# Fourteen experts on 64 slots with both parts of their tokens in one stationary tile, and gelu in one ScalarE pass

## What is computed

```python
logits = xf @ router_w + router_b            # 512 tokens, 32 experts
top_v, top_i = lax.top_k(logits, TOP_K)      # TOP_K = 4
gates = softmax(top_v)
# per expert, on its tokens:
gu = x_blk @ w_gu[e] + b_gu[e]               # 1024 -> 2048
gate = minimum(gu[:, :1024], 7.0)
up = clip(gu[:, 1024:], -7.0, 7.0)
act = (up + 1.0) * (gate * sigmoid(1.702 * gate))
y = act @ w_down[e] + b_down[e]              # 1024 -> 1024
# out: sum over a token's four experts of gate * y
```

## Time and profile before

| | |
|---|---|
| median of 3 runs | 1566.2 us (1562.85 to 1567.14) |
| span of the profiled execution | 1562.1 us |
| its own device time | not listed; its span lies 4.1 us below the median and 0.8 us below the fastest of the runs |
| TensorE busy | 1506.6 us, 96% |
| VectorE busy | 1380.6 us, 88% |
| ScalarE busy | 1006.1 us, 64% |
| GpSimd busy | 225.0 us, 14% |
| mean DMA rate over the span | 325 GB/s |

### The profile page before, as it was taken

How to read it: one execution, slowest core, us unless ns; L and a number is a source line. 1 busy time by engine, 2 the same in 40 slices (tenths; PEclk the granted TensorE clock), 3 DMA queues, 4 the chain that set the end, 5 groups by cost and what they waited for, 6 DMA issues and landing times.

```text
span 1562.1 us, 22575 instructions
## 1 busy us (share of the span) xinstructions
PE 1506.6 (96%) x8449; PEld 1179.3 (75%) x8449; DVE 1380.6 (88%) x1074; ACT 1006.1 (64%) x820; POOL 225.0 (14%) x236
## 2 busy tenths in 40 slices
PE   4999999998899999999999999999999999999996
PEld 2674468756688888888888888888888888888873
DVE  6888577487999999999999999999999999999997
ACT  4332433344577777777777777777777777777772
POOL 3343031000011111111111111111111111110061
PEclk9999999997999999999999999999999999999998
DMA  9788020216799999999999999999999999999992
GB/s 362 266 303 333 25 96 30 73 68 239 261 378 404 382 388 386 380 384 400 384 387 389 390 387 388 381 384 383 398 393 394 382 383 393 380 379 395 375 377 110
DMA packets 89144, 507.16 MB, mean 325 GB/s; under 512 B 11248, under 2 KB 12576, under 8 KB 37760
## 3 DMA queue, kind: packets, MB, share of 16 engines
q1 hardware_dynamic: 74256, 454.11, 74.3%
q0 software_dynamic: 9104, 34.08, 6.2%
q10 hardware_dynamic: 5728, 18.18, 2.9%
HBM read 477.51 MB, written 28.84 MB: 324 GB/s over the span
## 4 chain that ended last, share of the span: by engine, by line
PE 91%; DVE 5%; DMA 1%; ACT 1%; issue 1%; POOL 0%; SPq 0%; DVEq 0%; POOLq 0%; ACTq 0%
PE ps L2326 67%; PE ps L2342 2%; PE ps L1366 2%; PE ps L2305 2%; PE ps L1438 2%; PE ps L1352 2%; PE ps L1358 2%; PE ps L1355 2%; PE ps L1265 1%; DMA Wt<-in_ada_w 1%; PE ps L1360 1%; PE ps L2383 1%; PE ps L2315 1%; PE ps L2232 1%; PE ps L2249 1%
## 5 line engine op out<-in xcount | busy, mean ns | idle before, releaser
L1622 DVE TENSOR_TENSOR w_lo<-w_raw,w_hi 128x2048 fp32r<-128x2048 f32 x384 | 865.3, 2289 | 63.0 <-ACT w_hi L1616 59.2
L1616 ACT ACTIVATE w_hi<-w_raw 128x2048 fp32r<-128x2048 f32 x384 | 736.3, 1919 | 273.4 <-PE ps L2326 273.4
L2326 PE MATMUL ps<-w_hi,xTh 128*128 128x512 f32 x1024 | 406.2, 397 | 4.1 <-DVE xTl L2062 2.2
L2326 PE MATMUL ps<-w_lo,xTh 128*128 128x512 f32 x1024 | 400.0, 391 | 0.0
L2326 PE MATMUL ps<-w_hi,xTl 128*128 128x512 f32 x1024 | 275.0, 391 | 0.0
L2326 PEld LDWEIGHTS ps<-w_hi,xTh 128*128 128x128 f32 x1024 | 192.9, 188 | 51.2 <-issue 7.5
L2326 PEld LDWEIGHTS ps<-w_hi,xTl 128*128 128x128 f32 x1024 | 192.9, 188 | 40.5
L2326 PEld LDWEIGHTS ps<-w_lo,xTh 128*128 128x128 f32 x1024 | 192.8, 188 | 38.0
L2326 PE MATMUL ps<-w_hi,aTh 128*128 128x512 f32 x512 | 202.6, 396 | 0.0
L2326 PE MATMUL ps<-w_lo,aTh 128*128 128x512 f32 x512 | 199.5, 390 | 0.0
L1664 POOL TENSOR_TENSOR carried<-iotaE 128x1 f32<-128x1 f32 x64 | 27.9, 436 | 992.6 <-PE ps L2305 870.1
(11 more groups left out here) (425 smaller groups left out, 1590.6 us busy)
## 6 DMA issues: line engine op xcount, KB each, us to landing
w_raw<-in_moe_w_gu SPq DMA_DIRECT2D x256, 1024.0 KB, 6.6
w_raw<-in_moe_w_down SPq DMA_DIRECT2D x128, 1024.0 KB, 7.4
y_rows<-R ACTq DMA_DIRECT2D x30, 512.0 KB, 7.6
Wt<-in_ada_w SPq DMA_DIRECT2D x10, 1024.0 KB, 4.8
y_rows<-Wt POOLq DMA_DIRECT2D x1, 8704.0 KB, 24.6
Wt<-in_ada_w SPq DMA_DIRECT2D x16, 512.0 KB, 11.7
Wt<-in_w_in SPq DMA_DIRECT2D x4, 2048.0 KB, 9.7
R<-in_ada_w SPq DMA_DIRECT2D x6, 1024.0 KB, 8.3
```

The source lines that it names most:

```text
L1616: nc.scalar.activation(w_hi[:, at[-1] % HI_SLOTS, :], w_raw[:, at[-1] % RAW_SLOTS, :], ACT.Copy).then_inc(hi_rdy, 1)
L1622: nc.vector.tensor_tensor(w_lo[:, s, :], w_raw[:, s, :], w_hi[:, at[-1] % HI_SLOTS, :].bitcast(F32), ALU.subtract).then_inc(lo_rdy, 1)
L2326: ins = mm(ps[:, bank0 + c, :], x[:, k, :], w[:, 512 * (banks * i + c):512 * (banks * i + c) + 512], start=(first and i == 0 and x is xh a ...
```

## The change

Of the experts 2 to 29 the 14 with the fewest tokens are found on the chip, and they are called small here. The order of the steps is no longer that of the numbers: steps 3, 5, ... 29 are the small experts, the even steps from 2 to 28 the others; 0, 1, 30 and 31 stay. SyncE reads the number of each step's expert from SBUF before it loads. An expert is small up to 64 tokens and takes an overflow block beyond.

For a small expert the tokens' hi part stands in columns 0 to 63 of one stationary tile, their lo part in columns 64 to 127. One matmul with weight-hi and one with weight-lo give all four products, so a chunk has 8 matmuls instead of 12. The lower 64 rows of the sum belong on top of the upper ones: ScalarE copies them out of PSUM (`low_rows`, `low_rows_y`), TensorE adds them with a shifted identity (`fold`, four matmuls; `fold_y`, two).

For all experts the sigmoid becomes `Gelu_apprx_sigmoid`, one of swiglu's three instructions goes, and the activation of expert n is made in step n, ahead of c11, instead of at the start of step n+1. The bias takes eight matmuls instead of four. At the start, VectorE's `blocks` moves behind c3 of expert 0 and sorts the experts, `block_hots` and the list of tokens move into step 1, `overflows` into step 2. 4.7 MB more of `y_rows` are zeroed.

```diff
@@ constants
-MAXOV = 15
+MAXOV = 17
+SMALLS = 14
+DYN0, DYN1 = 2, E - 2
+TWO = 64
@@ GpSimd, constants, and the zeroing (L686)
             pool.dma_start(y_d[(E - 2) * BLK:NB * BLK, :].rearrange("(b p) d -> p b d", p=P),
                            zero_src.unsqueeze(1).to_broadcast([P, MAXOV + 2, D])).then_inc(y_zero, 16)
+            pool.dma_start(y_d[2 * BLK:(E - 2) * BLK, :].rearrange("(m q p) d -> q p m d", q=4, p=TWO)[3],
+                           zero_src[0:TWO].unsqueeze(1).to_broadcast([TWO, SMALLS, D])).then_inc(y_zero, 16)
@@ SyncE
+            sp.wait_ge(order_rdy, 1)
             with sp.Fori(1, E // 2) as m:
+                e = [sp.value_load(ordI[0:1, bass.ds(2 * m + k, 1)], min_val=0, max_val=E - 1) for k in (-1, 0, 1)]
                 for s in range(2):
                     for c in range(CHUNKS):
-                        load(sp, 2 * m + s if c < KT else 2 * m + (s - 1), c, lap(m, s, c))
+                        load(sp, e[s + 1] if c < KT else e[s], c, lap(m, s, c))
@@ ScalarE
+            def low_rows(gu_end):
                 wait_used(act, gu_end)
+                s_.activation(z_lo[TWO:P, :, :], ps[TWO:P, 0:4, :], ACT.Copy).then_inc(z_rdy, 1)
+            def low_rows_y(s, dn_end, stored):
                 wait_used(act, dn_end)
...
+                s_.activation(zy_lo[s][TWO:P, :, :], ps[TWO:P, 6:8, :], ACT.Copy).then_inc(z_rdy, 1)
@@ ScalarE, step
-                sigmoid(n - 1, before(KT - 1))
-                xt_evac(n, n)
+                xt_evac(n, by_place(n) if picked is None else picked, small)
                 for c in range(EARLY if yn is None else 0, 4):
                     split_hi(act, where(c))
+                    if c == 0 and small2:
+                        low_rows_y(s, before(CHUNKS - 1), stored)
...
                 if yn is not None:
-                    y_store(yn, s, before(CHUNKS - 1), stored)
+                    y_store(yn, s, before(CHUNKS - 1), stored, folded=nth - 1 if small2 else None)
                 for c in range(4, KT):
                     split_hi(act, where(c))
-                at_evac(n - 1)
-                for c in range(KT, CHUNKS):
+                at_evac(n - 1, small1)
+                for c in range(KT, CHUNKS - 1):
                     split_hi(act, where(c))
+                if small:
+                    low_rows(where(KT - 1))
+                    split_hi(act, where(CHUNKS - 1))
+                    gelu(n, where(KT - 1), nth)
+                else:
+                    gelu(n, where(KT - 1))
+                    split_hi(act, where(CHUNKS - 1))
@@ VectorE, before the steps
+            def sort_experts():
...
+                link(v.tensor_tensor(below, key[:, dyn].unsqueeze(1).to_broadcast([P, n, n]),
+                                     key[:, dyn].unsqueeze(2).to_broadcast([P, n, n]), ALU.is_lt))
+                link(v.tensor_reduce(rank_e[:, dyn], below, AX_X, ALU.add))
...
-            blocks()
             for c in range(KT):
                 split_lo(dve, place(0, c))
-                if c == 0:
+                if c == 2:
                     x_lo(0)
                 elif c == 3:
-                    block_hots()
+                    blocks()
@@ VectorE, beside
+                if (n, c) == (1, 1):
+                    expert_order()
+                elif (n, c) == (1, 2):
+                    block_hots()
...
+                elif (n, c) == (1, 5):
+                    dve.wait_ge(tok_mm, 2)
+                    v.tensor_copy(tok[:, 2:NB], ps[:, 7, S // 2 + 2:S // 2 + NB]).then_inc(tok_rdy, 1)
+                elif (n, c) == (2, 3):
+                    overflows()
@@ VectorE, swiglu and step
-                v.scalar_tensor_tensor(out=two(act_b), in0=ps[:, 0:2, :], scalar=LIMIT, in1=two(act_b), op0=ALU.min,
-                                       op1=ALU.mult).then_inc(act_rdy, 1)
...
-                swiglu(n - 1, before(KT - 1))
-                x_lo(n)
+                x_lo(n, small)
...
-                a_lo(n - 1)
-                for c in range(KT, CHUNKS):
+                a_lo(n - 1, small1)
+                for c in range(KT, CHUNKS - 1):
                     split_lo(dve, where(c))
+                swiglu(n, where(KT - 1), nth if small else None)
+                split_lo(dve, where(CHUNKS - 1))
@@ TensorE
+            def chunk_two(at, tiles, xt2, banks, bank0, first, last):
...
+                for i, k in enumerate(tiles):
+                    for c in range(banks):
+                        for part, w in enumerate((w_hi[:, hs, :], w_lo[:, ls, :])):
+                            ins = mm(ps[:, bank0 + c, :], xt2[:, k, :],
+                                     w[:, 512 * (banks * i + c):512 * (banks * i + c) + 512],
...
+            def fold(nth):
+                pe.wait_ge(z_rdy, 2 * nth - 1)
+                for c in range(4):
+                    ins = mm(ps[:, c, :], shift_up[TWO:P, :], z_lo[TWO:P, c, :], start=False, stop=True,
+                             skip_group_check=True)
+                ins.then_inc(fold_mm, 1)
@@ TensorE, step
                 pe.wait_ge(act_rdy, n)
-                bias(n, (half,))
+                bias(n, halves, small)
                 pe.wait_ge(xt_lo, n + 1)
                 for c in range(4):
-                    gate_up(where(c), c)
-                at_turn(n - 1)
+                    gate_up(where(c), c, small)
+                    if c == 1 and small2:
+                        fold_y(s, nth - 1)
+                at_turn(n - 1, small1)
                 for c in range(4, KT):
-                    gate_up(where(c), c)
+                    gate_up(where(c), c, small)
+                    if c == 4 and yn is None:
+                        pe.wait_ge(onehots, 2)
+                        tokens(block_p, block_t, ps[:, 7, S // 2:S // 2 + NB])
                 pe.wait_ge(at_lo, n)
                 if nxt is not None:
-                    xt(n + 1, 1 - s, nxt)
+                    xt(n + 1, 1 - s, nxt, small_next)
...
                 for c in range(4):
-                    down(where(KT + c), c)
+                    down(where(KT + c), c, small1)
+                    if c == 0 and small:
+                        fold(nth)
```

More of the change, by code:

```diff
@@ L1690, in _ @@
             pool.wait_ge(tok_rdy, 2)
-            with pool.Fori(1, E // 2) as m:
-                for s in range(2):
-                    gather(2 * m + s, s, 1)
+            with pool.Fori(1, E // 2 - 1) as m:
+                gather(2 * m, 0, 1)
+                gather(2 * m + 1, 1, 1, TWO)
+            for s in range(2):
+                gather(E - 2 + s, s, 1)
             def rows(t, which, ks, sem_in):
@@ L1826, in first_row @@
+            for n in range(2 * SMALLS + 2, E):
+                fixed_step(n, n // 2 - 1)
             def first_row(t):
@@ L2112, in beside, with step @@
                     tail_gates(n - 4)
-            def step(n, where, before, done=0, side=0):
-                swiglu(n - 1, before(KT - 1))
-                x_lo(n)
+            def step(n, where, small, small1, nth=None, done=0, side=0):
+                x_lo(n, small)
                 for c in range(KT):
@@ new lines, in fold_y, with at_turn @@
+            def fold_y(s, nth):
+                pe.wait_ge(z_rdy, 2 * nth)
+                for c in range(2):
+                    ins = mm(ps[:, 6 + c, :], shift_up[TWO:P, :], zy_lo[s][TWO:P, c, :], start=False, stop=True,
+                             skip_group_check=True)
+                ins.then_inc(fold_mm, 1)
+            def at_turn(n, small=False):
+                pe.wait_ge(act_rdy, n + 1)
+                turn(lambda k, rows: act_b[0:rows, 2 * P * (k // 2) + k % 2:2 * P * (k // 2 + 1):2], small
+                     ).then_inc(at_mm, 1)
@@ L2404, in _ @@
-            xt(1, 1, 1)
-            ov = overflow_count(pe)
-            at_step = lambda n: lambda c: place(n, c)
-            step(1, 1, at_step(1), 2, None, 0)
-            step(2, 0, at_step(2), 2, 1, 0)
-            step(3, 1, at_step(3), 3, 2, 0)
-            for half, (lo, hi) in enumerate(((2, HALF // 2), (HALF // 2, E // 2 - 1))):
-                with pe.Fori(lo, hi) as m:
-                    for s in range(2):
-                        step(2 * m + s, s, lambda c: lap(m, s, c), m + 1 + s, 2 * m + s - 1, half)
@@ L2414, in _ @@
-            step(E - 2, 0, at_step(E - 2), E // 2, E - 3, 1)
-            step(E - 1, 1, at_step(E - 1), None, E - 2, 1, True)
+            xt(1, 1, 1)
+            pe.wait_ge(gm_rdy, 1)
+            pe.wait_ge(tok_rdy, 1)
+            for t in range(TT):
+                for part in range(3):
+                    ins = mm(ps[E * part:E * part + E, 6, P * t:P * t + P], gm[:, t, :], ident[:], start=True, stop=True)
+            ins.then_inc(gmt_mm, 1)
+            at_step = lambda n: lambda c: place(n, c)
```

388 lines of the change are left out of this document (250 added, 138 removed).

## The result

The changed kernel takes 1574.4 us in the median of 5 runs (1570.8 to 1577.9), the kernel before 1565.8 us beside it (1562.9 to 1567.1). The ratio is 1.0058, with an interval of 1.0045 to 1.0072: **slower by 0.6%**. The profiled span grew from 1562.1 to 1572.6 us. I had forecast 1548 us, faster.

What follows compares the result with a forecast made beforehand. TensorE was taken to bound the kernel, VectorE and DMA close behind. Steps 3 to 30 at -26.6 us, start +6.5 and tail +1 gave -19 on the 1562.1 us span, 1543, median rounded 1548; range 1518 to 1576.

Steps and rivals of the forecast that it cites:

- What bounds the kernel before: Expert steps before the change: TensorE bounds them at 35.18 us a step, VectorE (32.69 us) and DMA (98%) close behind.
- The small step waits twice: Small step: VectorE waits for ScalarE 2.4 us before c1 and 1.9 before c4, making the step 35.4 us.
- with none: Pair of steps with neither of the small step's two VectorE waits: 64.2 us a pair, median 1487.
- the two waits shrink: Rival, chance 0.16: in small steps half of the 4.3 us of VectorE's waits goes; pair 66.3, median 1517.
- The rival on the other side: Rival, chance 0.14: TensorE's clock falls at c1 of small steps, losing 3 us a pair; pair 71.3, median 1587.
- The other step is bound by the four hi slots: Steps of the other experts: c10's hi part needs c6's slot, so the chain sums to 33.1 us a step.
- 0.3 of restarts: Other step: a term of some 0.3 us for restarts, beside the seven TensorE chunks of 2.73 us.
- The steps 3 to 30: 14 pairs of one small and one other step, each 68.5 us instead of 70.36: -26.6 us.
- The first pair: First pair of a small and another step: lacks the two waits on a result, which step 31 has instead.
- The start: Up to step 2: longer sorting and a late gather for expert 2 delay step 2 to near 465, +6.5 us (0 to 12).
- The tail: Step 31 to the end: last small result stored some 6 us later, moving the gathers behind it; +1 us (0 to 3).
- DMA binds: Rival, chance 0.12: transfers already full at 388 GB/s, 26.7 MB a pair take 68.9 to 70 us; 1554 to 1569.

Runs made afterwards that it cites:

- The gelu alone: The kernel before with only the one-pass gelu and the swiglu of two VectorE instructions instead of three: 1564.4 us, ratio 0.9991.
- the kernel with eight fillers: The changed kernel with eight throwaway matmuls on TensorE behind chunk 0 of each small step: 1562.7 us, ratio 0.9977.
- the late-fold kernel: The changed kernel with the copy, fold and store of a small expert's y moved later in all small steps but the last: 1502.5 us, ratio 0.9609.

## Why the prediction was wrong

- **What bounds the kernel before** was right: TensorE, with VectorE close behind. The gelu alone shows it.
- **"The small step waits twice"** was right in place and size: 35.4 us predicted, 35.48 read in step 15. Moving the two waits away gave 64.5 us a pair, where I had 64.2 for "with none". In the rival *the two waits shrink* I held the order in ScalarE's queue for fixed; it is three moved calls, and the largest gain here.
- **The clock, the step that failed first.** The forecast costed TensorE's wait of 2.57 us ahead of c1 at its length alone. The rival on the other side had it, at c1, but with 3 us a pair; it is 1.4 us a fall and falls in 9 of 13 steps, 12.3 us in all. My reason against it, that the known drop came behind 3.18 + 0.63 us, was a bound from a single row: 1.87 us is enough at times. The Trainium skill's TensorE: Matmul & The Clock Gate (Part 1), which I cited there, has the rule that an idle TensorE falls to the lower clock; the runs agree, behind 2.57 us in 9 places of 13 and behind 1.88 us in 7.
- **"The other step is bound by the four hi slots"** was right in kind and 0.7 us short: 69.28 - 35.48 = 33.80 us against 33.1. The chain in such a step, here step 20, and the start of VectorE's work behind the c11 before it:

```profile
1097.65 0.67 PE ps L2468 x5
1098.32 11.13 PE ps L2478 x48
1109.44 1.09 PE ps L2451 x8
1110.54 11.15 PE ps L2478 x48
```

```profile
1094.09 1.21 DVE L2196 TENSOR_TENSOR xTl<-ps,xTh 128x1024 fp32r<-128x1024 f32 x1
```

  Two terms were mis-sized. TensorE ends the last chunk 1097.65 - 1094.09 = 3.6 us behind VectorE's c11, where I had 3.0, and the transposes take 1.09, not 0.6. The chunks were right: 11.13 us for four is the 10.92 that I had and some of the 0.3 of restarts. The bias was costed too high, 0.67 against 0.9. The transposes are narrow here, as I had assumed, but that makes them no cheaper; eight of full width take 0.95 at this place in the earlier trace rows:

```profile
L2451 PE MATMUL ps<-ident,R x8: 270/280/332, 1109.3 to 1110.3; 64*128 64x64 f32 x7, 128*128 128x128 f32 x1
```

- **The steps 3 to 30 in all**, without the clock, are -19.3 us (the kernel with eight fillers), 7.3 above -26.6. The 13 pairs from step 5 on take 69.3 us and not 68.5, 11 us too much for my sum. The first pair takes 64.3, 4.2 less: it lacks the two waits, as the forecast says, but its sum has 14 pairs with them and leaves step 31 without. The 0.5 us left is rounding, since 70.36 - 68.5 is 1.86 and not 1.9.
- **The start**: +6.5 predicted, +11.1 measured. The idle stretch for the gather was as costed, 4 us. Not costed were GpSimd beside VectorE (the gather 4.9 us behind the list, not 1.5; its landing in 7.2 us instead of 10.5 gave most of it back) and a clock that falls behind that stretch: from the turn to step 2 it is 14.7 us, and 11.9 where the stretch was 1.37. That is 2.8 of the 4.6 us; 1.5 are the later start of expert 0, which I don't charge to the change.
- **The tail**: +1 predicted, +6.1 measured. "Some 6 us later" was right, the price wasn't. I let the store's delay end in the shade of other work, and didn't follow the chain: the store, three issues on GpSimd (2.84, 3.01 and 1.90 us), a gather of 11.36 us and `tail_add`, for which TensorE waits 2.38 us. The other 2.6 us are the two waits of 0.88 and 1.06 and the fold in step 31. The forecast had said that step 31 has such waits, and put no price on them there.
- **DMA binds**: no. The changed kernel moves 380 GB/s from 600 to 900 us, and the late-fold kernel 414 there. The Trainium skill's HBM Reference (Specifications), that one core alone goes well above its share of 358 GB/s, agrees.
- **The sign.** Clock 12.3, the pairs of steps 3 to 30 7.3, tail 5.1, start 4.6, step 2 0.3: 29.6 us above the sum I forecast, 1572.6 against 1543. Without the clock the kernel is at 0.9977 (0.9968 to 0.9986), faster by 0.2%. So the clock alone turns the sign, but no single term brings back the 1.1% that I had forecast: with any one of the first three at my value the kernel would still be within 0.4% of the one before.

## What to carry to other kernels

When a change takes the bounding engine's work away, write down each engine's queue again: an instruction that waited for nothing while its input was early may now stand ahead of everything. Put a copy that waits for another engine behind as much of its own engine's work as its buffer allows; here three moved calls were worth 4.5%. Price an idle stretch of TensorE at its length plus the slow matmuls behind it, and judge a part of the kernel by its own stretch of the trace when the rest varies.
